# A hybrid attention block on one core: the values of the differential attention projected for all heads ahead of the first head, seven weight tiles a head

## The reference

```python
hn = rmsnorm(h, g_norm[l]); proj = hn @ w_in[l]
aq, ak, av, ag, bq, bk, bv, bg, mq, mg = jnp.split(proj, IN_SPLITS, axis=-1)
a_out = swa_sink_attention(...)      # 8 heads of 64, window of 128 keys, sinks
# per block of 128 queries, 4 heads, two softmaxes each, keys of 64, values of 128:
logits = jnp.einsum('bqchd,bschd->bchqs', qb, k) * scale - slopes * dist   # masked by chunk
p = jax.nn.softmax(logits, axis=-1); attn = p[:, 0] - lam * p[:, 1]
b_heads = jnp.einsum('bhqs,bshd->bqhd', attn, v)      # v = bv, the values of this case
b_out = rmsnorm(b_heads, b_subln_g[l]) * (1.0 - lam_init)
m_out = memory_attention(...)        # 4 heads of 128, 256 memory rows, keys and values memn @ w_mem_kv
gated = concat([a_out * silu(ag), b_out * silu(bg), m_out * silu(mg)])
y = rmsnorm(h + gated @ w_out[l], g_final)
```

## Time and profile before

| | |
|---|---|
| median of 3 runs | 704.76 us (704.73 to 705.06) |
| the profiled execution's own time | 704.69 us |
| its span | 702.9 us |
| PE busy | 692.9 us, 99% |
| DVE, ACT, POOL busy | 420.1 (60%), 311.8 (44%), 231.4 us (33%) |
| the chain that ended last, PE's part | 91% |
| transfers | 52.73 MB, mean 75 GB/s |
| granted clock of PE, mean | 0.999 |

### The profile page before, as it was taken

The page is one execution under the profiler, slowest core; times in us unless marked ns, Lnnn a source line. Parts: engine busy times, 40 slices in busy tenths (PEclk is TensorE's granted clock), DMA queues, the critical chain, the costliest instruction groups (busy, mean ns, idle before and its releaser), DMA issues.

```text
span 702.9 us, 11709 instructions
## 1 busy us (share of the span) xinstructions
PE 692.9 (99%) x3989; PEld 582.3 (83%) x3989; DVE 420.1 (60%) x922; ACT 311.8 (44%) x729; POOL 231.4 (33%) x204
## 2 busy tenths in 40 slices
PE   8999999999999999999999999999999999999996
PEld 8988888888888888888888888888888887888885
DVE  6786246766754666675466667635667786433332
ACT  7753444455543444564344556334454654122200
POOL 5723132144333214333331434233243543222310
PEclk9999999999999999999999999999999999999999
DMA  9921212020052101005211110421140285514210
GB/s 298 309 62 30 61 32 60 1 60 2 1 151 61 40 21 43 19 1 151 61 30 31 31 31 1 146 65 30 31 124 5 61 273 153 158 60 129 81 59 37
DMA packets 79158, 52.73 MB, mean 75 GB/s; under 512 B 36081, under 2 KB 71937, under 8 KB 79105
## 3 DMA queue, kind: packets, MB, share of 16 engines
q1 hardware_dynamic: 79104, 52.06, 25.8%
HBM read 43.14 MB, written 8.91 MB: 74 GB/s over the span
## 4 chain that ended last, share of the span: by engine, by line
PE 91%; DVE 6%; ACT 2%; issue 1%; DVEq 0%; POOL 0%; ACTq 0%; POOLq 0%
PE acc L1490 18%; PE acc L1491 17%; PE acc L1492 17%; PE score L1490 4%; PE score L1492 3%; PE score L1491 3%; PE trans L1492 3%; PE trans L1490 3%; PE trans L1491 3%; PE score L1684 2%; PE score L1686 2%; PE trans L1704 2%; PE mixo L1491 2%; DVE logits L1393 2%; PE mixo L1492 2%; PE mixo L1490 2%
## 5 line engine op out<-in xcount | busy, mean ns | idle before, releaser
L1490 PE MATMUL acc<-x_hi,w_hi 128*128 128x512 f32 x544 | 217.3, 400 | 0.2 <-DVE gates L1258 0.2
L1491 PE MATMUL acc<-x_lo,w_hi 128*128 128x512 f32 x544 | 212.8, 391 | 0.0
L1492 PE MATMUL acc<-x_hi,w_lo 128*128 128x512 f32 x544 | 212.5, 391 | 0.0
L926 POOL TENSOR_TENSOR w_lo<-w_raw,w_hi 128x512 fp32r<-128x512 f32 x66 | 85.0, 1308 | 175.4 <-ACT w_hi L604 156.6
L1492 PEld LDWEIGHTS acc<-x_hi,w_lo 128*128 128x128 f32 x544 | 102.1, 188 | 22.2
L1490 PEld LDWEIGHTS acc<-x_hi,w_hi 128*128 128x128 f32 x544 | 102.3, 188 | 20.6 <-issue 1.9
L1491 PEld LDWEIGHTS acc<-x_lo,w_hi 128*128 128x128 f32 x544 | 102.4, 188 | 17.9
L773 ACT ACTIVATE logits<-logits,stats_b 128x128 f32<-128x128 f32 (+7 forms) x64 | 49.2, 770 | 50.4 <-DVE stats_b L1287 50.4
L1279 DVE CUSTOM_DVE_ANT_0 logits<-score,b_bias 128x384 f32<-128x384 f32 (+5 forms) x96 | 50.0, 554 | 23.1 <-PE score L1686 22.6
L782 ACT ACTIVATE p_hi<-trans 128x512 fp32r<-128x512 f32 (+1 forms) x56 | 30.8, 565 | 63.4 <-PE trans L1704 42.1
L1306 DVE TENSOR_TENSOR p_lo<-trans,p_hi 128x512 fp32r<-128x512 f32 (+1 forms) x56 | 35.8, 651 | 33.6 <-ACT p_hi L782 33.2
(11 more groups left out here) (249 smaller groups left out, 1359.3 us busy)
## 6 DMA issues: line engine op xcount, KB each, us to landing
w_raw<-in_w_in SPq DMA_DIRECT2D x68, 256.0 KB, 3.4
mixed<-gates SPq DMA_DIRECT2D x9, 512.0 KB, 4.2
mix_raw<-mixed SPq DMA_DIRECT2D x8, 576.0 KB, 5.8
wo_raw<-in_w_out SPq DMA_DIRECT2D x8, 512.0 KB, 6.7
x_res<-in_x SPq DMA_DIRECT2D x8, 512.0 KB, 3.4
out_y<-y_row SPq DMA_DIRECT2D x16, 256.0 KB, 2.1
logits<-in_x SPq DMA_DIRECT2D x4, 512.0 KB, 7.9
wo_raw<-in_w_out SPq DMA_DIRECT2D x6, 256.0 KB, 5.9
```

What stands on the lines that cost most here:

```text
L926: last = pool.tensor_tensor(w_lo[:, slot, cols], w_raw[:, slot, cols], w_hi[:, slot, cols].bitcast(F32), ALU.subtract)
L1490: pe.matmul(out, a_hi, b_hi, start=start, stop=False, skip_group_check=True)
L1491: pe.matmul(out, a_hi, b_lo, start=False, stop=False, skip_group_check=True)
L1492: return pe.matmul(out, a_lo, b_hi, start=False, stop=stop, skip_group_check=True)
```

## The change

The tile bv is gone from `TILES`, and a head has seven tiles. Ahead of the heads, behind the shared tiles, PE projects the values of all four heads at once (`value_tile`): x is now the loaded side and 512 columns of w_in stream, so each bank has 128 rows of the sequence by 512 value columns, already the way the mix wants them. Eight banks collect over four weight tiles; ACT and DVE copy four banks each to `v_all` (the memory of `logits`), SP stores them to `values` in the chip's memory, and for each head loads its 128 columns into `v_in` (the memory of `b_out`). There ACT and POOL split them (`v_split`). The memory's values are made the same way around (`mem_value_tile`), so their transposes go; the memory's keys and values are stored to `mem_kv` and loaded per head, since their place now holds the split mq, which so far lay over the scores' q. The outer loops of ACT, DVE, POOL and SP are written out. `BETWEEN` is redone for 40 quarters behind tile 1's end instead of 48; the second tile carries `v_split` and `mkv`. The order of the steps among themselves is kept, but for `b_squares(0)`, now ahead of `a_mix(1)`. What stands between them are fewer quarters, and `evacuate` and `weights` fall at other places among them.

```diff
-TILES = [("bk", BK, True), ("bq", BQ, True), ("bv", BV, False), ("aq", AQ, True), ...
+TILES = [("bk", BK, True), ("bq", BQ, True), ("aq", AQ, True), ("ag", AG, True), ...
...
 BETWEEN = {
+    (1, 0, 0): [("v_split", 0)],
+    (1, 0, 2): [("v_split", 1)],
+    (1, 1, 0): [("mkv",)],
...
-    (3, 0, 0): [("b_scores", 2, 0)],
-    (3, 0, 1): [("b_scores", 3, 0), ("b_combine", 2)],
+    (2, 1, 3): [("b_scores", 2, 0)],
+    (3, 0, 0): [("b_scores", 3, 0), ("b_combine", 2)],
...
+            def value_tile(n):
+                pe.wait_ge(w_lo_done, n + 1)
+                for t in range(ST):
...
+                    rows = slice(t * P, (t + 1) * P)
+                    for c in range(2):
+                        k = 2 * (n - OWN_TILES) + c
+                        cols = slice(c * HALF, (c + 1) * HALF)
+                        last = product(v_banks[t], x_hi[:, k, rows], x_lo[:, k, rows], w_hi[:, n % 2, cols],
+                                       w_lo[:, n % 2, cols], k == 0, k == KT - 1)
...
-                def v_spread(half):
...
-                    for j in range(4):
-                        cols = slice((4 * half + j) * P, (4 * half + j + 1) * P)
-                        last = pe.transpose(out[:, j * P:(j + 1) * P], bv_t[:, cols], ident[:, :])
...
+                def v_split(half):
+                    ts = slice(4 * half, 4 * half + 4)
+                    act.wait_ge(v_loaded, 16 * (h + 1))
+                    act.wait_ge(pt_done, h * NMIX)
+                    act.activation(v_hi[:, ts, :], v_in[:, ts, :], ACT.Copy).then_inc(v_hi_done, 1)
...
+            def load_values(h):
+                if h == 0:
+                    sp.wait_ge(v_stored, 16 * ST)
+                sp.dma_start(v_in, values_v[:, :, h * P:(h + 1) * P]).then_inc(v_loaded, 16)
...
-            with sp.Fori(0, HEADS - 1) as h:
-                for w in range(2, NT + 2):
+            for h in range(HEADS - 1):
+                for w in range(2 if h else 3, NT + 2):
                     load_head_tile(w, h)
-                for g in "amb":
+                for g in "am":
                     spill(g, h)
+                load_mem_kv(h + 1)
+                spill("b", h)
+                load_values(h + 1)
...
-            sp.wait_ge(mkv_lo, 2 * HEADS)
-            load_mix(0, 0)
             sp.wait_ge(s_full, at(S_AT[("b", 7, 1, 1)], H, NS))
             load_wo(1)
             load_wo(2)
+            sp.wait_ge(s_full, NS * HEADS)
+            load_mix(0, 0)
```

More of the change, by code:

```diff
@@ L66 @@
[L66 to L90, removed]
+    (2, 1, 0): [("b_combine", 1)],
@@ new lines @@
+    (4, 0, 3): [("b_scores", 6, 0), ("b_spread", 2, 2), ("b_mix", 2, 0), ("b_mix", 2, 1), ("b_scores", 6, 1)],
+    (4, 1, 0): [("b_scores", 7, 0), ("a_spread", 0), ("b_scores", 7, 1)],
+    (4, 1, 1): [("a_scores", 1)],
+    (4, 1, 2): [("b_combine", 6)],
+    (4, 1, 3): [("b_combine", 7)],
+    (5, 0, 0): [("a_norm", 1), ("b_mix", 2, 2)],
+    (5, 0, 2): [("b_spread", 3, 0), ("b_spread", 3, 1), ("a_scores", 2), ("a_mix", 0), ("a_spread", 1), ("m_scores", 0), ("a_norm", 2)],
+    (5, 0, 3): [("b_spread", 3, 2)],
@@ new lines @@
+    (5, 1, 0): [("b_mix", 3, 0), ("m_norm", 0)],
+    (5, 1, 1): [("b_spread", 3, 3), ("b_mix", 3, 1), ("b_fold", 0)],
+    (5, 1, 2): [("b_mix", 3, 2), ("m_spread", 0), ("b_mix", 3, 3), ("m_scores", 1), ("b_low", 0)],
+    (5, 1, 3): [("b_squares", 0), ("a_mix", 1), ("m_norm", 1), ("a_scores", 3), ("m_scores", 2), ("a_spread", 2)],
+    (6, 0, 0): [("a_norm", 3), ("m_spread", 1), ("m_norm", 2), ("m_mix", 0)],
+    (6, 0, 1): [("m_scores", 3), ("b_fold", 1)],
+    (6, 0, 2): [("a_mix", 2), ("m_norm", 3), ("m_spread", 2)],
@@ L91 @@
+    (6, 0, 3): [("m_mix", 1), ("b_low", 1)],
+    (6, 1, 0): [("m_spread", 3), ("m_mix", 2)],
+    (6, 1, 1): [("a_spread", 3), ("m_mix", 3), ("b_squares", 1)],
+    (6, 1, 2): [("b_finish", 0)],
+    (6, 1, 3): [("b_finish", 1), ("b_gate",), ("a_mix", 3)],
 }
@@ L877, in head @@
                         wo_hi_part(s[1])
-            with act.Fori(0, HEADS - 1) as h:
+            for h in range(HEADS - 1):
                 head(h, HEAD)
@@ L938, in pre_lo_half @@
                                           ALU.subtract)
-            for n in range(PRE_TILES):
+            for n in range(OWN_TILES):
                 if n > 0:
@@ L1029, in head @@
                             .then_inc(wo_lo_by_pool, 1)
-            with pool.Fori(0, HEADS - 1) as h:
+            for h in range(HEADS - 1):
                 head(h, HEAD)
@@ L1450, in head @@
                         mix_mid_part(s[1])
-            with dve.Fori(0, HEADS - 1) as h:
+            for h in range(HEADS - 1):
                 head(h, HEAD)
```

327 lines of the change are left out of this document (206 added, 121 removed).

## The result

The kernel with values ahead of the heads takes 755.56 us (median of 4 runs, 752.78 to 756.07) against 704.75 (4 runs, 704.46 to 705.06): ratio 1.071, 95% interval [1.069, 1.072], slower by 51 us. The forecast was slower, 736.0 us, and the time lies above its range (712 to 750). The profiled run took 755.77 us with a span of 754.0; before, 704.69 and 702.9.

A forecast was written before the change was run, and what follows sets the result against it. PE's instruction stream was taken to bound the kernel: 704.69 - 5.0 removed work + 28.4 waits inside four heads + 7.8 waits at the starts of heads 1 to 3 = 735.9 us, forecast as 736; 8-in-10 range 712 to 750.

The forecast's parts named there:

- Removed work: On PE, value transposes in heads and memory go and the memory's value product uses fewer matmuls: 5.0 us saved.
- busy time would fall by 5: Sign to look for: PE's busy time should fall by about 5 us.
- A: Turned probabilities of pair 1 (b_spread 1): PE waits behind b_combine(3), 1.4 us a head, bounds 0 and 2.2.
- B: b_spread 2: PE waits behind b_combine(5), delayed by a gate half's evacuation on DVE; 3.0 us a head, bounds 1.5 and 3.5.
- C: b_spread 3: PE waits behind b_combine(7), three quarters of cover instead of five; 0.6 us a head, bounds 0 and 1.2.
- D: b_squares(0), now ahead of a_mix(1), its former cover: 0.5 us wait a head, bounds 0 and 0.6.
- E: m_spread 2: PE waits behind m_norm(2), with the next tile's split ahead on POOL; 1.6 us a head, bounds 0 and 2.4.
- F: Start of heads 1 to 3: tile 2 lands later and v_hi delays q's evacuation; 2.6 us each, 7.8 in all, bounds 2.7 and 11.4.
- The end: End of the last head, a quarter less under its gates and splits: 0 us, bounds 0 and 1.5.
- The clock: Rival, chance 0.10: waits of near 3 us lower PE's clock in the heads, 1.5 us per fall; 746 to 752 us.

The follow-up runs named there:

- e13_mix: e4_all with v_split behind the q evacuation, further weight splits, turns and copies reordered, and m_mix(1) a quarter earlier; 706.36 us.
- e4_all: Kernel after with the edits of e1_b and e2_f, weight splits of tiles 4, 6 and 7 later, a_mix(1) ahead of b_squares(0); 716.54 us.
- e1_b: Kernel after with b_combine(4) ahead of the evacuation of gate half (3, 1) and b_combine(5) ahead of a_scores(0) on VectorE; 742.76 us.
- e5_c: e3_busy with the weight split of tile 6 behind a_norm(1) instead of at the start of tile 5; 737.40 us.
- e6_e: e3_busy with the weight split of tile 7 behind m_norm(2) instead of at the start of tile 6; 740.12 us.
- e10_q: e7_v without added matmuls at the head starts, next head's tile 2 loaded behind the spills but ahead of the reads; 731.82 us.
- e7_v: e3_busy with both v_split behind the evacuation of q, and 8 instead of 14 added matmuls at the starts of heads 1 to 3; 738.42 us.
- e3_busy: Kernel after with unread matmuls added in PE's waits: 14 at tile 2 of heads 1 to 3, 10 ahead of each b_spread(2, 0); 742.51 us.
- e11_ad: e3_busy with the weight split of tile 4 behind b_combine(3) and a_mix(1) ahead of b_squares(0); 738.01 us.
- e12_last: e13_mix with a_scores(0) also moved behind b_spread(2, 1) and a_norm(0) behind the two b_mix of group 2; 718.42 us.
- e2_f: Kernel after with tile 2 of the next head loaded ahead of the spills and reads; 737.37 us.

## Why the prediction was wrong

**Removed work, -5.0:** not refuted, but not seen whole. The sum above closes to 0.2 us with it; by e13_mix a head saves some 0.6 us less than the rows said. That busy time would fall by 5 was wrong: it rose by 10.7. The matmuls at half clock count twice as long, and the last one ahead of each wait is counted at its full 0.39. But in e13_mix too, with no fall of the clock, it fell only from 692.9 to 691.9.

**A, 1.4:** measured 1.22. Right in the total, by luck in the parts. With the split moved away 0.42 stays (e4_all), where the prediction's cover of 2.8 against 2.2 left nothing; the queue's part is 0.8 instead of 2.0.

**B, 3.0 (bounds 1.5 and 3.5):** measured 2.44 to 2.81. Right, with its cause (e1_b).

**C, 0.6 (bounds 0 and 1.2):** measured 1.48, outside the bounds. I kept the durations of before. Under the new order POOL's weight split falls on b_combine(7), and that alone adds 0.95 (e5_c). The 0.5 us left there is the 0.6 of the prediction.

**D, 0.5:** 0.62. **E, 1.6:** 1.20, by the queue named (e6_e). A to E in all: 7.0 us a head, forecast 7.1. That the total fits is luck, C's miss (0.9) was made good by E and B (0.4 each).

**F, 2.6 in each of three heads:** 3.85, 2.90, 4.43, so 11.2 instead of 7.8. The mechanism was right in both parts, the queue (e10_q) and ScalarE (e7_v). The size was short: 0.75 MB at 263 GB/s made 2.9 us of delay, and the reads cost 3.6 to 4.0 (e10_q); and the prediction took 2.6 as a middle value, though its own parts added up to 3.8, near the 3.7 that the three waits have in the mean.

**The end, 0 (bounds 0 and 1.5):** 0.9, by the same kind of meeting of DVE and POOL as C.

**Left out:** the 0.16 us that each wait costs beside its idle time, 3.7 us for A to F.

**The clock.** This is the step that failed. It stood beside the forecast as a rival with a chance of 0.10, and what spoke against it was that the earlier trace rows shows the fall only behind a longer pause. That row says that a long pause is enough and nothing of a shorter one. At six of the seven waits of 2.4 us and more the clock fell, and 11.9 us were lost (e3_busy). The rival's size, 10 to 16 us on top of the forecast, was right, though made of other places: it had falls behind A and E too, at 1.5 us each, where there was none, and behind two of the F waits the loss was 2.9 and 2.7. So the mechanism was seen and priced, and given the wrong chance. The waits of A to F, forecast at 36.2 us, measured 39.4 idle and 43.1 lost; with them and no fall of the clock the kernel is at 742.5 (e3_busy), inside the range. From the forecast's 735.9 the clock (11.9), the 0.16 at each wait (3.7), F (3.4) and the end (0.9), less 0.2 at A to E, lead to 755.6. The Trainium skill (TensorE: Matmul & The Clock Gate, HAM oscillation — how this bites in real kernels) was cited in the prediction for waits between bursts that lower the clock again and again. The trace agrees with that. The page's own case has waits of some 3 to 5 us; here 2.44 us were enough. I should have put the loss into the sum as soon as the sum contained such waits.

## What to carry over

When a sum puts waits of some 2.5 us or more on TensorE, price the clock in the same sum: here a fall was worth 1.6 to 2.9 us beyond the wait's length, and the six together 11.9 of 51 us. Filling the wait with matmuls that nobody reads gives that part back and separates it from the wait. And when cover shrinks, do not keep the old durations: look at which VectorE and GpSimd instructions with SBUF inputs now fall together, and expect a part of what a reordering removes to come back one place on, here nothing (e5_c), a quarter (e11_ad) or half of it (e1_b, e6_e).

## What the hardware showed that I had not expected

- The granted clock was at 1.2 GHz for 3.41 or 6.83 us at waits of 2.44 to 4.43 us (the kernel after), and at waits of 2.7 us in e12_last. At waits of up to 1.6 us it stayed at 2.4 GHz in every profile here. Nearly the same wait had a fall in some heads and executions (2.44, 2.81 in the kernel after) and none in others (2.45 in head 0 there, 2.80 in e2_f), which alone moves a run by 1.6 us.
- A VectorE instruction of 1.28 us took 2.23 and one of four columns 1.22 instead of 0.16 beside a GpSimd subtraction; the GpSimd pair took 3.49 instead of 2.54. At the end of the last head it was 1.87 instead of 0.69.
- PE's idle time understates a wait by 0.16 us: the record of the last 512-column matmul is 0.39 us, the step to the next start 0.227.
